# Moving one VectorE instruction in the seven-product blocks of a hybrid encoder's second layer

## What is computed

```python
for l in range(2):
    proj = _rmsnorm(x, norm1_g[l]) @ w_in[l]
    branch_a = attention(proj) @ w_attn_up[l]
    branch_b = gated(gelu(state_space(proj)) @ w_glu[l])
    x = x + (gate_a * branch_a + gate_b * branch_b) @ w_o[l]
    n = _rmsnorm(x, norm2_g[l])
    x = x + (silu(n @ w_ffn_gate[l]) * (n @ w_ffn_up[l])) @ w_ffn_down[l]
```

## Time and profile before

| | us |
|---|---|
| median of 3 runs | 1540.43 (1538.33 to 1541.2) |
| profiled execution | 1544.6 |
| its span (first to last instruction) | 1542.8 |
| TensorE busy | 1496.2 |
| VectorE busy | 1090.7 |
| ScalarE busy | 670.1 |
| GpSimd busy | 425.8 |

### The profile page before, as it was taken

The page is one execution under the profiler, slowest core; times in us unless marked ns, Lnnn a source line. Parts: engine busy times, 40 slices in busy tenths (PEclk is TensorE's granted clock), DMA queues, the critical chain, the costliest instruction groups (busy, mean ns, idle before and its releaser), DMA issues.

```text
span 1542.8 us, 23041 instructions
## 1 busy us (share of the span) xinstructions
PE 1496.2 (97%) x8954; PEld 1225.2 (79%) x8954; DVE 1090.7 (71%) x1491; ACT 670.1 (43%) x1146; POOL 425.8 (28%) x232
## 2 busy tenths in 40 slices
PE   8999999999999999999999999899999999999998
PEld 3555887778788878888888888887888988988997
DVE  5999888677448986658423871686788875886684
ACT  4463158742452232233333223688336541553351
POOL 0000053454443455444443323445440000000000
PEclk9999999999999999999999999999999999999999
DMA  6568720232242254453538632003331242224123
GB/s 245 161 202 300 284 72 1 67 104 76 96 138 82 90 171 139 152 155 96 167 96 295 207 134 89 28 1 109 97 109 57 83 143 76 83 83 150 66 86 123
DMA packets 73500, 189.52 MB, mean 123 GB/s; under 512 B 23600, under 2 KB 32176, under 8 KB 69296
## 3 DMA queue, kind: packets, MB, share of 16 engines
q1 hardware_dynamic: 41952, 145.18, 28.3%
q10 hardware_dynamic: 31440, 42.87, 8.6%
HBM read 155.52 MB, written 32.51 MB: 122 GB/s over the span
## 4 chain that ended last, share of the span: by engine, by line
PE 61%; DVE 20%; DVEq 5%; DMA 5%; ACT 4%; issue 4%; POOLq 1%; POOL 1%; SPq 0%; ACTq 0%
PE ps L2148 18%; PE ps L2150 18%; PE ps L2149 18%; DVE wl L1994 3%; DMA stage_more<-in_stream 2%; DMA stage<-in_stream 2%; PE ps L2297 2%; PE ps L2274 1%; DVE work L1377 1%; PE ps L2203 1%; DVEq L1557 1%; DVEq L1986 1%; ACT prob L1143 1%; DVE wsum L1979 1%; DVEq L1504 1%
## 5 line engine op out<-in xcount | busy, mean ns | idle before, releaser
L632 POOL TENSOR_TENSOR wl<-stage,wh 128x1024 fp32r<-128x1024 f32 x138 | 356.7, 2592 | 648.9 <-ACT wh L725 459.3
L725 ACT ACTIVATE wh<-stage 128x1024 fp32r<-128x1024 f32 (+2 forms) x178 | 181.0, 1023 | 226.1 <-PE ps L2150 104.6
L2148 PE MATMUL ps<-XH,wh 128*128 128x256 f32 x616 | 176.6, 287 | 14.4 <-DVE wl L1994 7.3
L2150 PE MATMUL ps<-XH,wl 128*128 128x256 f32 x616 | 173.7, 282 | 0.0
L2149 PE MATMUL ps<-XLr,wh 128*128 128x256 f32 x528 | 148.7, 282 | 0.0
L2148 PE MATMUL ps<-xg2h,wh 128*128 128x512 f32 x352 | 140.2, 398 | 0.0
L2150 PE MATMUL ps<-xg2h,wl 128*128 128x512 f32 x352 | 139.2, 395 | 0.0
L2149 PE MATMUL ps<-xg2l,wh 128*128 128x512 f32 x352 | 139.2, 395 | 0.0
L2148 PEld LDWEIGHTS ps<-XH,wh 128*128 128x128 f32 x616 | 116.7, 189 | 20.0 <-DVE wl L1994 11.4
L2150 PEld LDWEIGHTS ps<-XH,wl 128*128 128x128 f32 x616 | 116.9, 190 | 0.0
L2203 PE MATMUL ps<-X,slabs 128*128 128x512 f32 x224 | 101.7, 608 | 6.7 <-DMA X<-in_xT 5.2
(11 more groups left out here) (346 smaller groups left out, 3660.1 us busy)
## 6 DMA issues: line engine op xcount, KB each, us to landing
stage<-in_stream SPq DMA_DIRECT2D x178, 512.0 KB, 3.5
stage_more<-in_stream SPq DMA_DIRECT2D x34, 512.0 KB, 3.9
CPTR<-ctd_scr ACTq DMA_DIRECT2D x6, 1664.0 KB, 8.8
slabs<-in_stream SPq DMA_DIRECT2D x17, 512.0 KB, 5.5
InT<-in_scr ACTq DMA_DIRECT2D x6, 1024.0 KB, 7.0
ctd_scr<-CPp SPq DMA_DIRECT2D x4, 1152.0 KB, 7.8
ctd_scr<-CPp ACTq DMA_DIRECT2D x4, 1152.0 KB, 6.5
in_scr<-BPI SPq DMA_DIRECT2D x4, 1024.0 KB, 5.0
```

What stands on the lines that cost most here:

```text
L632: pool.tensor_tensor(wl[:, s, :], stage[:, (n - RAW) % STAGES, :], wh[:, s, :].bitcast(F32), ALU.subtract).then_inc(wl_ready, 1)
L725: return act.activation(o, i, ACT.Copy, **kw)
L2148: pe.matmul(o, wt[0], x[0], start=start, stop=False, skip_group_check=onto)
L2150: return pe.matmul(o, wt[1], x[0], start=False, stop=stop, skip_group_check=onto)
```

## The change

In VectorE's list corner_low(q) moves from the end to the place behind first_sum(q), so ahead of low(0, q+1), sums_last(q+1), scaled(q-1) and low(1, q+1), and in the last block of a part ahead of the two down_low. Nothing else changes.

```diff
                     if q < last:
                         sums_first(q + 1)
                     first_sum(q)
+                    corner_low(q)
                     if q < last:
                         low(0, q + 1)
                         sums_last(q + 1)
@@ -2111,7 +2112,6 @@
                         low(1, q + 1)
                     else:
                         down_low(h, 1)
-                    corner_low(q)
                     if q == 0:
                         dve.wait_ge(rms_ready, 2 * l + 2)
                         dve.reciprocal(rscol[:], rscol[:]).then_inc(rs_ready, 1)
```

## The result

The changed kernel takes 1525.48 us (median of 4 runs, 1524.97 to 1526.54) against 1540.82 for the kernel before: ratio 0.9901, interval 0.9882 to 0.9919, so 12.5 to 18.2 us less. The forecast was 1526.8, in a range of 1522 to 1533. The profiled execution took 1525.92, its span 1524.1.

What follows compares the result with a forecast made beforehand. TensorE was taken as held by VectorE and the slab buffer's late release, losing 18.1 us. Less 4.5 us of waits left, the gain is 13.6: 1540.4 - 13.6 = 1526.8 us, range 1522 to 1533 (own range 1524.5 to 1529, chance 0.64).

Steps and rivals of the forecast that it cites:

- The bound: Second-layer blocks: TensorE loses 18.1 us to waits over thirteen blocks, 147.3 us against 129.2 at 9.94 each.
- the loop corner_low, slab, sums_first: VectorE frees the slab's buffer, SP reloads it, the weight sum needs it: 11.4 us a block, 6.4 after the change.
- The price of the new wait: On VectorE, corner_low(q) must now wait for ScalarE's high3, which needs P4(q-1); everything queued behind it waits too.
- floor of 6.83: Earliest start of corner_low(q), in us after its block's first matmul: high3 ends at 6.78, plus 0.05.
- the handover from ScalarE: Delay from high3's end to VectorE's corner_low, taken as 0.05 us, with ends 0.03 and 0.15.
- The walk: Starts followed through two blocks until they close: 19.88 + 0.39 = 20.27 us a pair, against 22.8 today.
- Waits left: TensorE waits remaining: 8 x 0.39 = 3.1 us at P4 behind even blocks, 1.4 at part ends, together 4.5.
- The sum: Whole kernel: gain 18.1 - 4.5 = 13.6 us, median 1540.4 to 1526.8.
- Rival 2: VectorE instructions resumed behind a semaphore lose the 0.08 overlap, so the new wait costs 7 us more: 1534; chance 0.17.
- Rival 1: All waits vanish and TensorE alone sets 9.94 us a block: 1522.3; chance 0.12.
- Rival 3: SP has another wait ahead of the slab's load, so nothing moves: 1540.4; chance 0.03.
- Rival 4: ScalarE falls behind by d a block, corner_low holds VectorE's list, a pair takes 20.1 + 2d: 1545; chance 0.04.

Runs made afterwards that it cites:

- late_release: Changed kernel, but SP loads the second slab of block q+2 only after low1(q+1) has ended too; 1542.18 us, ratio 1.0037 to the kernel before.
- untied: Kernel before, old order, with the corner operand also loaded into three own buffers, freeing the slab's buffer earlier from the third block; 1523.75 us, ratio 0.9922.
- after_sums: Changed kernel with corner_low behind sums_last(q+1), in a part's last block behind down_low(h, 0); 1521.20 us, ratio 0.9884 to the kernel before.
- high3_late: Changed kernel with ScalarE's rounding of the corner (high3) moved behind its copy of P6; 1553.32 us, ratio 1.0115 to the kernel before.
- before_low1: Changed kernel with corner_low moved between scaled(q-1) and low1(q+1); 1520.83 us, ratio 0.9884 to the kernel before.
- after_again: The changed kernel run once more, unaltered, on the chip of the last two placements; 1529.34 us, ratio 0.9922 to the kernel before.
- rest_later: Changed kernel with rest(q-2) behind other_sums(q-1) in odd blocks instead of ending the even blocks' list; 1525.38 us, ratio 0.9941 to the kernel before.

## Why the prediction was right, point by point

- **The bound.** 18.1 us lost to waits, through the loop corner_low, slab, sums_first: shown from both sides by late_release (order without release, 12.3 of the 13.5 us lost again) and untied (release without order, 16.9 us). The 9.94 us of the prediction are block 9 alone, not blocks 9 and 10; block 10 takes as long.
- **The price of the new wait.** The floor of 6.83 was met within 0.01, and the handover from ScalarE, bounded by 0.03 and 0.15 and taken as 0.05, lies at the lower bound: high3(2) ends at 1197.84 + 0.63 = 1198.47 and corner_low(2) starts at 1198.50, 0.03. ScalarE's rows for this, the corner copy and high3(2) as in the earlier trace rows:

```profile
1197.56 0.39 ACT L725 ACTIVATE up<-ps 128x256 f32<-128x256 f32 x1 [0.95 <-PE ps L2150]
1197.84 0.63 ACT L725 ACTIVATE wh<-stage_more 128x512 fp32r<-128x512 f32 x1
```

- **The walk.** Two blocks were to take 20.27; blocks 11 to 14 start at 1328.04 and end at 1368.55, which is 20.26 a pair:

```profile
1328.04:1368.55 40.51, 40.24 (x338) 39.89 (x337) 38.45 (x51) 22.98 (x36) 0.00 (x0) 1.00 0.32 104
```

- **Waits left.** 4.5 us were forecast. The windows hold 132.55 - 129.22 = 3.3, forecast 3.1: eight times 0.37 (the walk's 0.31 and 0.07 make 0.38, not 0.39), and 0.3 behind one idle time of VectorE that the walk didn't have (last section). P4(7) starts 1254.75 - 1252.78 = 1.97 behind the first of the down steps instead of 1.41: 0.56, forecast 0.55.
- **The sum.** 13.6 us forecast, 13.5 in the stretch. The medians differ by 15.3; the 13.5 lie in their interval of 12.5 to 18.2, and between the two profiled executions the rest lies ahead of block 1 (last section).
- **Rival 2**, that an instruction resumed behind a wait loses its overlap, falls: corner_low(2), resumed at 1198.50, lasts 0.69, and low0 starts 0.61 behind it. The Trainium skill, VectorE: DVE Perf Modes, section The DRAIN you can't avoid, has the next operation wait until the pipe is empty, but adds in the same paragraph that a next operation which is not held starts earlier. The 0.61 is such an earlier start, so the trace bears out the addition; the prediction set the trace against the first half alone, and "This trace disagrees" is too strong.
- **Rival 1** (all waits vanish) needed corner_low to be free of high3 but for the last blocks, as in after_sums. I named what spoke against it, but not that a later place would have met it. **Rival 3** (no release) falls with the waits of L1979.
- **Rival 4** has its mechanism right and its price too low. By its 20.1 + 2d a pair takes 22.94 at the tested d of 1.42, and it took 22.95, hardly more than the 22.8 of the kernel before; yet the stretch of high3_late is 12.8 us longer than that of the kernel before. I counted eight pairs inside the parts; the thirteen blocks of the earlier trace rows hold only 2.7 of the 12.8. Another 4.9 lie in the first blocks of the parts, which in the old order lose nothing, while the loop through high3 binds from a part's third block on (11.2 us instead of 9.94); and 5.2 lie at the parts' ends, where P4 of the last block starts 2.9 to 3.2 us behind the first down step instead of 1.4. The Trainium skill, PSUM — Partial Sum Buffer, section Engine vs sequencer instructions, calls VectorE's queue strict FIFO; high3_late agrees, with everything behind L1999 held by 1.2 to 1.5 us in each block inside a part.

## What to carry to other kernels

An instruction that frees a buffer belongs early enough that the loop through its load is shorter than the bound, and no earlier: moved too far, it meets its own operand and holds its whole queue. Write the loops as sums of starts from the trace, with the floor that each semaphore sets, and walk two periods until they close; here this told TensorE's waits behind an even block and at a part's end to 0.02 us. The size of an engine's wait in the profile says little about its cost until a loop through it is longer than the bound. In before_low1 10.4 us of DMA waits cost 0.4. In the changed kernel 7.6 us of corner_low's waits for ScalarE, in blocks 1, 8, 9, 16 and 17, cost nothing (these blocks take as long in after_sums), while waits of 0.07 to 0.24 us in eight even blocks mark the loop that costs eight times 0.37.

## What the runs showed of the hardware that I had not expected

TensorE's instructions ahead of block 1, the same in all nine kernels, take between 1180.0 and 1188.9 us in these profiles. Part of it is TensorE's clock. Windows at 880 us of the kernel before and of the changed one:

```profile
880.00:895.00 15.00, 14.26 (x159) 13.18 (x158) 8.01 (x17) 2.69 (x4) 2.41 (x1) 0.77 0.51 185
```

```profile
880.00:895.00 15.00, 14.26 (x222) 12.57 (x222) 11.07 (x18) 3.75 (x5) 3.35 (x2) 1.00 0.64 236
```

The granted clock was full in the one and 0.77 on the mean, so part of the time at 1.2 GHz, in the other, with 159 matmuls done instead of 222. The matmuls of the first window take 11.9 us in the changed kernel (879.11 to 891.03), so this place makes 3.1 of the 5.2 us between the two. What decides on the clock there was not tried. Only a stretch that starts behind such places compares two kernels to a tenth of a microsecond.

One more row stays unexplained. In block 6 VectorE idles ahead of scaled(5) with nothing to wait for that the profile shows:

```profile
1242.65 1.23 DVE L2084 TENSOR_TENSOR up<-up,act 128x1024 f32<-128x1024 f32 x1 [0.44 <-issue]
```

The same 0.44 stands at the same instruction in all six kernels in which corner_low stands ahead of scaled (also late_release, after_again, rest_later, high3_late and after_sums), and in none of the three in which it stands behind it. It made P5(7) and P4(6) wait a little longer in the changed kernel, 0.3 us together; in after_sums it cost TensorE nothing. Its cause was not tried.
